# The final RMSNorm of a two-group decoder step: from feature columns to token rows

## The chip, the cores and the metric

One core of one Trainium2 chip. The metric is the device time of one execution of the whole program in microseconds (us); the median of several executions counts. Engines are named as in the profile: PE (TensorE), DVE (VectorE), ACT (ScalarE), POOL (GpSimd), SP (SyncE, which only issues DMAs here).

## What is computed

One step of a decoder layer for two groups that share the weights: a prompt of 512 tokens and 8 sample sequences with one new token each, so T = 520 tokens, model width 1024. The layer has three mixers (sparse attention, a short convolution, a linear recurrence), an output projection and a SwiGLU feed-forward of width 2816. At its very end stands the part that the change touches:

```python
xp = xp + _swiglu(_rmsnorm(xp, norm2_g[l]), w_ffn_in[l], w_ffn_out[l])
...
y_prompt = _rmsnorm(xp, final_g)     # x * rsqrt(mean(x*x, -1) + eps) * final_g, for each token
y_sample = _rmsnorm(xs, final_g)
```

All outputs are float32. Each dense product is made of three products of rounded halves (high x high, high x low, low x high), so every k step of every weight tile issues six matmuls.

## The kernel before, in words

The residual stream lives in SBUF with the features on the partitions: `xT` is [128, 8 feature tiles, 520 tokens]. Weights come in chunks of 256 output columns. For each chunk SP issues two DMAs into one of two raw buffers (`load`), ACT copies it rounded (`hi`, line 821), POOL subtracts the rounded copy (`split`, line 729), and PE multiplies (`dense`, its matmuls at line 1770). In `dense` a chunk has two output tiles, m = 0 and 1, and for each the k steps of 128 input features follow one another; a hook `between(m, k)` can put other PE work behind a k step. In an earlier stage this hook already carries turns of the same kind: `kv_turn`, lines 2037 and 2038, four 128x128 transposes and one of 8 rows between k steps.

The last stage of weights is the output product of the feed-forward, chunks `C_FO` = 70 to `C_END` = 82. An output pair is 12 chunks in two rounds of a PE loop (`pe.Fori(0, 2)`), each with j = 0 to 5: j = 0 to 2 sum over the 22 feature tiles of the hidden layer (8, 8 and 6 k steps) into the PSUM tiles D[0] and D[1], j = 3 to 5 the same for two more output tiles into the four banks of E. DVE adds each finished tile to the residual (`xT`, line 1749, semaphore `x_last`), ACT squares it (line 828) and DVE adds the square to `rstd`, which here serves as the sum of squares (line 1134).

The final norm follows the last tile, each step waiting for the one before:

- PE multiplies the sum of squares with a matrix of 1/1024 (`norm_sums(2)`), which leaves the mean of every token on all 128 partitions.
- ACT takes the square root of 128x520 (line 834), DVE the reciprocal (line 1118).
- DVE scales the eight tiles with the column of `final_g` and the token row (line 1123) into `yT`.
- PE turns `yT` by 128 tokens at a time into D[0] and D[1], then the 8 sample tokens into E (lines 2239 and 2243); ACT and DVE copy half of each turned block to `y_tok[q]` (lines 1096, 1757, 1760).
- SP stores 128 tokens with a DMA as soon as both halves are there, and the sample rows last (line 467, 2.13 MB in five DMAs).

`yT` lies in SBUF where the hidden layer's activations are still read until the last matmul.

Of the kernel before, what the change touches and what calls it, by code (L numbers as in the profile page):

```python
# [44 lines left out]
FT = D_FF // P  # L45
# [15 lines left out]
C_Q, C_KV, C_GM0, C_NSA, C_WO, C_FI, C_FO, C_END = 26, 30, 36, 40, 44, 48, 70, 82  # L61
# [17 lines left out]
def build(nc, x_prompt, x_sample, cache_kv, cache_win, state_sconv, state_lru_conv, state_lru_h, page_table,  # L79
# [4 lines left out]
    with ExitStack() as ctx:  # L84
        def sem(name):
            return ctx.enter_context(nc.semaphore(name))
# [23 lines left out]
        xT = sb("xT", [P, KT, T])  # L110
# [13 lines left out]
        g_cols = sb("g_cols", [P, 3, KT])  # L124
# [155 lines left out]
        y_tok = [over(f"y_tok{q}", [P, D_MODEL]) for q in range(QT)]  # L280
        ys_tok = over("ys_tok", [NS, D_MODEL])
        yT = over("yT", [P, KT, T])

        D = [ctx.enter_context(nc.psum_tensor(f"D{m}", [P, 2, 512], F32)) for m in range(2)]
        E = ctx.enter_context(nc.psum_tensor("E", [P, 4, 512], F32))
# [6 lines left out]
        off_blk = smalls[:, 5, 0:NS * NBLK_S]  # L292
        o_all = tmp[:, 0, 0:KVC].rearrange("p (g d) -> p g d", g=N_KV)
        o_own = tmp[:, 1, 0:2 * DH]

        x_landed = [sem(f"x_landed{q}") for q in range(QT)]
# [40 lines left out]
        v_hi = sem("v_hi")  # L338
        v_lo = sem("v_lo")
        neg_la = sem("neg_la")  # L340
        la_exp = sem("la_exp")
        mult_sq = sem("mult_sq")
        mult_ready = sem("mult_ready")
        y_sq = sem("y_sq")
        gelu_arg = sem("gelu_arg")
        gelu_tanh = sem("gelu_tanh")
# [84 lines left out]
        x_last = sem("x_last")  # L431
        y_ready = sem("y_ready")
        y_turned = sem("y_turned")
        y_evac_a = sem("y_evac_a")
        y_evac_v = sem("y_evac_v")

        block = ctx.enter_context(nc.Block())

# [24 lines left out]
        def _(sp):  # L463
            outs = [0]

            def out(dst, src):
                sp.dma_start(dst, src).then_inc(out_written, 16)
                outs[0] += 16
# [171 lines left out]
            with sp.Fori(0, 2) as i:  # L640
                for j in range(6):
                    k0, nk = ((0, KT), (KT, KT), (2 * KT, FT - 2 * KT))[j % 3]
                    load(C_FO + 6 * i + j, j % 2, wk[:, k0:k0 + nk, bass.ds(i * 2 * CW + (j // 3) * CW, CW)], nk)
            for q in range(QT):
                sp.wait_ge(y_evac_a, q + 1)
                sp.wait_ge(y_evac_v, q + 1)
                out(y_prompt[0, q * P:(q + 1) * P, :], y_tok[q][:, :])
            sp.wait_ge(y_evac_v, QT + 2)
            out(y_sample[:, 0, :], ys_tok[:, :])
            sp.wait_ge(out_written, outs[0])  # L650
            sp.wait_ge(rows_moved, 3 * 16)

# [142 lines left out]
        def pair(ap):  # L796

            return ap.rearrange("p (a c) -> p a c", a=2)
# [14 lines left out]
        def _(act):  # L813
# [16 lines left out]
            def norm(k):  # L830

                act.wait_ge(sq_summed, k)
                sums = D[0][:, :, 0:HALF] if k == 2 else E[:, 0:2, 0:HALF]
                nc.scalar.activation(pair(tmp[:, 0, :]), sums, ACT.Sqrt, bias=eps_col[:, 0:1])\
                    .then_inc(rms_done, 1)
            act.dma_start(xs_in[:, :], x_sample[:, 0, :]).then_inc(xs_landed, 16)
            for n, g in enumerate((norm1_g[0], norm2_g[0], final_g)):
# [48 lines left out]
                if ft % 2 == 1:  # L886
                    hi(4, ft // 2)
            act.wait_ge(neg_la, WT)
            nc.scalar.activation(la[:, :, :], t0[:, :, :], ACT.Exp, scale=-1.0).then_inc(la_exp, 1)
            nc.scalar.activation(lm[:, :, :], t0[:, :, :], ACT.Tanh).then_inc(la_exp, 1)  # L890
            hi(5, 0)
            act.wait_ge(mult_sq, 1)
            nc.scalar.activation(lm[:, :, :], lm[:, :, :], ACT.Sqrt).then_inc(mult_ready, 1)
            hi(5, 1)
            def mix(i, c0):

# [187 lines left out]
            for c in range(C_FO, C_END):  # L1084
                if c < C_END - 2:
                    hi((c + 2) // 2, c % 2)
                if c % 3 == (C_FO + 2) % 3:
                    for m in range(2):
                        n = (c - C_FO) // 3 * 2 + m
                        act.wait_ge(x_last, 4 + n + 1)  # L1090
                        square(2, n)
            norm(2)

            for q in range(QT):
                act.wait_ge(y_turned, q + 1)
                nc.scalar.activation(y_tok[q][:, 0:512], D[q % 2][:, 0, :], ACT.Copy).then_inc(y_evac_a, 1)

        @block.vector
        def _(dve):  # L1100
# [7 lines left out]
            def settle():  # L1108
                dve.wait_ge(vec_step, steps[0])
# [6 lines left out]
            def norm(k):  # L1116
                dve.wait_ge(rms_done, k)
                step(nc.vector.reciprocal(rstd[:, :], tmp[:, 0, :]))
                settle()
                if k < 2:  # L1120
                    return
                for ft in range(KT):
                    nc.vector.scalar_tensor_tensor(yT[:, ft, :], xT[:, ft, :], g_cols[:, k, ft:ft + 1],  # L1123
                                                   rstd[:, :], ALU.mult, ALU.mult).then_inc(y_ready, 1)

            def clear_squares():
                step(nc.vector.memset(rstd[:, :], 0.0))

            def add_square(k, ft, parity):

                n = KT * (k - 1) + ft
                dve.wait_ge(sq_done, n + 1)
                dve.wait_ge(sq_added, n)
                nc.vector.tensor_tensor(rstd[:, :], rstd[:, :], tmp[:, parity, :], ALU.add).then_inc(sq_added, 1)
# [159 lines left out]
            dve.wait_ge(la_exp, 2)  # L1294
            step(nc.vector.tensor_tensor(t0[:, :, :], la[:, :, :], la[:, :, :], ALU.mult))
            settle()

# [5 lines left out]
            dve.wait_ge(mult_ready, 1)  # L1303
            step(nc.vector.memset(lm[:, :, 0:1], 1.0))
            step(nc.vector.memset(la[:, :, 0:1], 0.0))
            settle()
# [434 lines left out]
                gated(i, 1)  # L1741

            clear_squares()
            settle()
            for n in range(KT):
# [12 lines left out]
            dve.wait_ge(y_turned, QT + 1)  # L1758
            for k in range(2):
                nc.vector.tensor_copy(ys_tok[:, k * 512:(k + 1) * 512], E[0:NS, k, :]).then_inc(y_evac_v, 1)  # L1760

        @block.tensor
        def _(pe):
            mm, turn = nc.tensor.matmul, nc.tensor.transpose

            def product(out2, lhsT, rhs, first, last):

                for a in range(2):
                    ins = mm(out2[:, a, 0:HALF], lhsT, rhs[:, a * HALF:(a + 1) * HALF], start=first, stop=last)  # L1770
                return ins
# [40 lines left out]
            def norm_sums(k):  # L1812

                pe.wait_ge(sq_added, KT * k)
                product(D[0] if k == 2 else E[:, 0:2, :], ones[:, :], rstd[:, :], True, True).then_inc(sq_summed, 1)

            for m in range(2):
# [398 lines left out]
                    dense(2 * i + b, b, KT, xgH, xgL)  # L2217
            for m in range(2):
                pe.wait_ge(tile_free[m], 1 + C_FO)
            with pe.Fori(0, 2) as i:  # L2220
                for j in range(6):
                    if j < 3:
                        pe.wait_ge(act_lo, 2 + min((j + 1) * KT, FT))
                    if j % 3 == 0:
                        pe.wait_ge(x_last, 4 * i + 2 + 2 * (j // 3))
                    outs = [D[0], D[1]] if j < 3 else [E[:, 0:2, :], E[:, 2:4, :]]
                    nk = KT if j % 3 < 2 else FT - 2 * KT
                    part = min(j % 3, 1)
                    dense(6 * i + C_FO + j, j % 2, nk, actH[part], actL[part], x0=(j % 3 - part) * KT, outs=outs,
                          first=(j % 3 == 0), last=(j % 3 == 2))  # L2230
            norm_sums(2)
            for q in range(QT):
                if q >= 2:
                    pe.wait_ge(y_evac_a, q - 1)
                    pe.wait_ge(y_evac_v, q - 1)
                for ft in range(KT):
                    if q == 0:
                        pe.wait_ge(y_ready, ft + 1)
                    ins = turn(D[q % 2][:, ft // 4, (ft % 4) * P:(ft % 4 + 1) * P], yT[:, ft, q * P:(q + 1) * P],
                               ident[:, :])  # L2240
                ins.then_inc(y_turned, 1)
            for ft in range(KT):
                ins = turn(E[0:NS, ft // 4, (ft % 4) * P:(ft % 4 + 1) * P], yT[:, ft, SEQ:T], ident[:, :])
            ins.then_inc(y_turned, 1)
# [27 lines left out]
```

## Time and profile before

| what | value |
|---|---|
| time, median of 3 runs | 1195.12 us (1194.12 to 1198.5) |
| time of the profiled execution | 1197.33 us |
| its span, first to last instruction | 1195.6 us |
| mean granted TensorE clock | 0.981 |
| busy: PE, DVE, ACT, POOL | 1134.1, 469.5, 372.5, 467.0 us |
| DMA moved in all | 126.28 MB, mean 106 GB/s |

### The profile page before, as it was taken

The page shows a single profiled execution, that of the slowest core. Times are in us where ns is not written, and L with a number is a line of the kernel's source. Part 1 is how long each engine was busy: PE and PEld are TensorE (multiplying, and loading weights), DVE is VectorE, ACT ScalarE, POOL GpSimd, SP SyncE. Part 2 cuts the span into 40 slices and gives each one's busy share as a digit, 9 for nine tenths or more (in the row PEclk, how much of TensorE's full clock was granted, in tenths as well). Part 3 has the DMA queues.
Part 4 walks back from the last instruction along what each step waited for, and adds up shares of the span by engine and source line. Part 5 has one row for each costly group of instructions (what it writes and reads, how often), then busy time and mean ns, then how long its engine had stood idle before and what let it go on. Part 6 is the DMA issues. An engine that isn't in the chain of part 4 may idle for free.

```text
span 1195.6 us, 20737 instructions
## 1 busy us (share of the span) xinstructions
PE 1134.1 (95%) x8502; PEld 1043.1 (87%) x8502; DVE 469.5 (39%) x618; ACT 372.5 (31%) x497; POOL 467.0 (39%) x265
## 2 busy tenths in 40 slices
PE   5899989999999999899899889999999999999995
PEld 5899989999999988765454579999999999999994
DVE  5586583123421230557662624352332233200115
ACT  5113433322211225255545313342322222212211
POOL 5333455555443423215511133444434344344440
PEclk9899999999999999999999989999999999999997
DMA  5532117324622223442116573223232322222201
GB/s 172 167 104 73 53 53 227 104 75 123 195 74 83 90 75 113 160 134 52 33 42 221 162 264 106 84 94 101 76 105 71 104 95 80 96 71 98 97 26 72
DMA packets 109362, 126.28 MB, mean 106 GB/s; under 512 B 10670, under 2 KB 102982, under 8 KB 107775
## 3 DMA queue, kind: packets, MB, share of 16 engines
q1 hardware_dynamic: 105784, 120.19, 32.2%
q10 hardware_dynamic: 3527, 5.39, 1.4%
q8 instruction: 35, 0.57, 0.2%
q14 instruction: 16, 0.13, 0.0%
HBM read 111.38 MB, written 16.17 MB: 107 GB/s over the span
## 4 chain that ended last, share of the span: by engine, by line
PE 75%; issue 13%; POOL 5%; DVE 3%; DMA 2%; ACT 1%; SPq 0%; ACTq 0%; POOLq 0%; DVEq 0%
PE D L1770 55%; PE E L1770 6%; PE D L2021 5%; POOL w_lo L729 4%; PE D L2006 1%; PE D L2007 1%; DMA w_raw<-in_w_in 1%; DVE nmax L1484 1%; PE E L1987 1%; PE E L2077 1%; PE E L1956 1%; DMA slot<-in_cache_win 1%; PE E L1982 0%; PE E L2037 0%; DVE yT L1123 0%
## 5 line engine op out<-in xcount | busy, mean ns | idle before, releaser
L729 POOL TENSOR_TENSOR w_lo<-w_raw,w_hi 128x1024 fp32r<-128x1024 f32 x164 | 402.0, 2473 | 565.4 <-ACT w_hi L821 544.5
L821 ACT ACTIVATE w_hi<-w_raw 128x1024 fp32r<-128x1024 f32 x164 | 164.1, 1049 | 300.1 <-PE D L1770 243.6
L1770 PE MATMUL D<-hH,w_hi 128*128 128x260 f32 x1152 | 239.9, 290 | 7.6 <-POOL w_lo L729 5.5
L1770 PE MATMUL D<-hH,w_lo 128*128 128x260 f32 x1152 | 233.5, 285 | 0.0
L1770 PE MATMUL D<-hL,w_hi 128*128 128x260 f32 x1152 | 233.5, 285 | 0.0
L1770 PEld LDWEIGHTS D<-hH,w_hi 128*128 128x128 f32 x1152 | 179.9, 191 | 12.5 <-POOL w_lo L729 5.7
L1770 PEld LDWEIGHTS D<-hL,w_hi 128*128 128x128 f32 x1152 | 179.4, 190 | 0.0
L1770 PEld LDWEIGHTS D<-hH,w_lo 128*128 128x128 f32 x1152 | 179.3, 190 | 0.0
L1770 PE MATMUL D<-onH,w_lo 128*128 128x260 f32 x816 | 164.5, 283 | 0.0
L1770 PE MATMUL D<-onH,w_hi 128*128 128x260 f32 x816 | 164.3, 282 | 0.0
L1770 PE MATMUL D<-onL,w_hi 128*128 128x260 f32 x816 | 164.2, 283 | 0.0
L1770 PEld LDWEIGHTS D<-onH,w_hi 128*128 128x128 f32 x816 | 125.9, 188 | 0.1
L1770 PEld LDWEIGHTS D<-onH,w_lo 128*128 128x128 f32 x816 | 125.8, 188 | 0.0
L1770 PEld LDWEIGHTS D<-onL,w_hi 128*128 128x128 f32 x816 | 125.4, 188 | 0.0
L2021 PE MATMUL D<-pT,vst 128*128 128x512 f32 x160 | 83.3, 605 | 2.3 <-ACT obuf L1016 2.3
L1007 ACT ACTIVATE pT<-D 128x512 f32<-128x512 f32 x80 | 47.4, 596 | 65.9 <-PE D L2007 65.8
L2006 PE MATMUL D<-qst,k 128*128 128x512 f32 x80 | 60.6, 757 | 5.4 <-issue 3.4
L779 POOL TENSOR_SCALAR_AFFINE_SELECT pT<-pT 128x512 f32<-128x512 f32 x32 | 23.6, 736 | 105.8 <-ACT pT L1007 105.8
L1484 DVE TENSOR_REDUCE nmax<-E 128x2 f32<-128x256 f32 (+3 forms) x64 | 51.1, 822 | 20.9 <-PE E L1983 13.6
L1729 DVE TENSOR_TENSOR tmp<-D,th 128x520 f32<-128x520 f32 x22 | 15.4, 699 | 88.3 <-PE D L1770 88.3
L1075 ACT ACTIVATE actH<-tmp 128x520 f32 x22 | 14.1, 640 | 93.3 <-DVE tmp L1729 93.3
L1719 DVE TENSOR_TENSOR D<-D,rstd 128x520 f32<-128x520 f32 x22 | 15.6, 707 | 64.4 <-PE D L1770 64.2
(357 smaller groups left out, 1490.8 us busy)
## 6 DMA issues: line engine op xcount, KB each, us to landing
w_raw<-in_w_in SPq DMA_DIRECT2D x64, 512.0 KB, 5.0
w_raw<-in_w_ffn_in SPq DMA_DIRECT2D x44, 512.0 KB, 4.1
slot<-in_cache_kv SPq DMA_DIRECT2D x64, 128.0 KB, 2.6
w_raw<-in_w_ffn_out SPq DMA_DIRECT2D x16, 512.0 KB, 4.0
rows_b<-rnorm_d SPq DMA_DIRECT2D x8, 512.0 KB, 4.7
w_raw<-in_w_nsa_out SPq DMA_DIRECT2D x8, 512.0 KB, 9.0
slot<-in_cache_win SPq DMA_DIRECT2D x16, 256.0 KB, 4.6
w_raw<-in_w_o SPq DMA_DIRECT2D x8, 512.0 KB, 4.2
```

What stands on the lines that cost most here:

```text
L729: nc.gpsimd.tensor_tensor(wl[b][:, x], raw[b][:, x], wh[b][:, x].bitcast(F32), ALU.subtract)\
L779: nc.gpsimd.affine_select(out=p, in_=p, compare_op=ALU.is_ge, fill=0.0, base=0, pattern=[[0, R], [1, P]], channel_multiplier=-1).then_inc( ...
L821: nc.scalar.activation(wh[b][:, x], raw[b][:, x], ACT.Copy).then_inc(hi_done, 1)
L1007: nc.scalar.activation(pT[t % 4][:, :, :].rearrange("p r x -> p (r x)"), D[0][:, t % 2, :], ACT.Exp)\
L1075: nc.scalar.activation(actH[part][:, bass.ds(2 * i - part * KT + m, 1), :].squeeze(1), tmp[:, m, :], ACT.Copy).then_inc(act_hi, 1)
L1484: nc.vector.reduce_max(nmax[:, g % 2, a, :, qi % 2, h], src, AX.X, negate=True).then_inc(nmax_done, 1)
L1719: nc.vector.tensor_tensor(o, o, pair(rstd[:, :]), ALU.mult).then_inc(ffn_gate, 1)
L1729: nc.vector.tensor_tensor(pair(tmp[:, m, :]), D[m][:, :, 0:HALF], pair(th[:, m, :]), ALU.mult)\
L1770: ins = mm(out2[:, a, 0:HALF], lhsT, rhs[:, a * HALF:(a + 1) * HALF], start=first, stop=last)
L1956: mm(E[:, ft % 4, :], vbig[:, ft * P:(ft + 1) * P], pcT[:, :, :].rearrange("p q x -> p (q x)"), start=True, stop=True).then_inc(cmp_out, 1)
L2006: mm(out, k1[b][:, br, ks], qst[b][:, qi, :, :].rearrange("p r x -> p (r x)"), start=True, stop=False)
L2021: mm(D[1][:, i % 2, :], vst[g % 2][:, br, kt, :], pT[t % 4][:, :, :].rearrange("p r x -> p (r x)"), start=(kt == 0), stop=(kt == qi)).then ...
```

## The change

The final norm is taken token by token, with tokens on the partitions. The unscaled residual tiles are turned while the last output products still run: a turn of tile n writes the four blocks of 128 tokens into one bank of D[0] and the 8 sample tokens into a bank of D[1], alternating two banks. DVE multiplies the turned tile with `g_row`, `final_g` spread over all partitions by a DMA from SP, into `y_tok` and `ys_tok` (`weigh`). Turns 0 to 3 stand behind k = 0, 2, 4, 6 of the second tile of chunk j=3 of the second round, turns 4 and 5 in the first tile of j=4, turn 6 behind k=3 of the second tile of j=5, and turn 7 follows the last matmul. The PE loop is written out for this. The sums of squares come as one column for each block of 128 tokens (`token_sums`, one matmul per block with the squares as weights and one column of 1/1024), first for the sum of tiles 0 to 6, then added for tile 7 from its own square. Square root and reciprocal are then of 128x5. Whole rows are scaled last, in place: DVE takes blocks 0 and 2 and the sample rows, SP stores them; ACT takes blocks 1 and 3 and stores them from its own queue. A dummy square root behind ACT's first weight copies of this stage loads the activation table. `y_tok`, `ys_tok` and `g_row` lie where the input of the feed-forward was, free by then. Two pairs of semaphores are merged into one each, as is said in the diff.

```diff
+        y_tok = over("y_tok", [P, QT, D_MODEL])
         ys_tok = over("ys_tok", [NS, D_MODEL])
-        yT = over("yT", [P, KT, T])
+        g_row = over("g_row", [P, D_MODEL])
...
+        rms_y, rstd_y = smalls[:, 1, 0:QT + 1], smalls[:, 2, 0:QT + 1]
...
-        la_exp = sem("la_exp")
+        la_act = sem("la_act")
-        mult_ready = sem("mult_ready")
...
# SP
-            for q in range(QT):
-                sp.wait_ge(y_evac_a, q + 1)
-                sp.wait_ge(y_evac_v, q + 1)
-                out(y_prompt[0, q * P:(q + 1) * P, :], y_tok[q][:, :])
-            sp.wait_ge(y_evac_v, QT + 2)
+            sp.wait_ge(pe_done, 2 * C_FO)
+            sp.dma_start(g_row[:, :], final_g.unsqueeze(0).to_broadcast([P, D_MODEL])).then_inc(g_landed, 16)
+            for n, q in enumerate((0, 2)):
+                sp.wait_ge(y_scaled_v, n + 1)
+                out(y_prompt[0, q * P:(q + 1) * P, :], y_tok[:, q, :])
+            sp.wait_ge(y_scaled_v, 3)
             out(y_sample[:, 0, :], ys_tok[:, :])
-            sp.wait_ge(out_written, outs[0])
+            sp.wait_ge(out_written, outs[0] + 2 * 16)
...
# ACT
+                if c == C_FO:
+                    nc.scalar.activation(smalls[:, 3, 0:1], eps_col[:, :], ACT.Sqrt)
-            norm(2)
-
-            for q in range(QT):
-                act.wait_ge(y_turned, q + 1)
-                nc.scalar.activation(y_tok[q][:, 0:512], D[q % 2][:, 0, :], ACT.Copy).then_inc(y_evac_a, 1)
+            act.wait_ge(sq_summed, 2)
+            nc.scalar.activation(rms_y[:, 0:QT], E[:, :, 0:1].squeeze(2), ACT.Sqrt, bias=eps_col[:, 0:1]).then_inc(rms_done, 1)
+            nc.scalar.activation(rms_y[0:NS, QT:QT + 1], D[0][0:NS, 0, 0:1], ACT.Sqrt, bias=eps_col[0:NS, 0:1])\
+                .then_inc(rms_done, 1)
+            act.wait_ge(y_ready, 1)
+            act.wait_ge(y_weighed, KT)
+            for n, q in enumerate((1, 3)):
+                nc.scalar.activation(y_tok[:, q, :], y_tok[:, q, :], ACT.Copy, scale=rstd_y[:, q:q + 1])\
+                    .then_inc(y_scaled_a, 1)
+                act.wait_ge(y_scaled_a, n + 1)
+                act.dma_start(y_prompt[0, q * P:(q + 1) * P, :], y_tok[:, q, :]).then_inc(out_written, 16)
...
# DVE
-                for ft in range(KT):
-                    nc.vector.scalar_tensor_tensor(yT[:, ft, :], xT[:, ft, :], g_cols[:, k, ft:ft + 1],
-                                                   rstd[:, :], ALU.mult, ALU.mult).then_inc(y_ready, 1)
...
+            step(nc.vector.memset(rms_y, 1.0))
...
+            def weigh(n):
+                dve.wait_ge(y_turned, n + 1)
+                x = slice(n * P, (n + 1) * P)
+                nc.vector.tensor_tensor(y_tok[:, :, x], D[0][:, n % 2, :].rearrange("p (q x) -> p q x", q=QT),
+                                        g_row[:, x].unsqueeze(1).to_broadcast([P, QT, P]), ALU.mult)
+                nc.vector.tensor_tensor(ys_tok[:, x], D[1][0:NS, n % 2, 0:P], g_row[0:NS, x], ALU.mult)\
+                    .then_inc(y_weighed, 1)
+
+            for n in range(6):
+                last_tile(n)
                 if n > 0:
                     add_square(2, n - 1, (n - 1) % 2)
-            add_square(2, KT - 1, 1)
-            norm(2)
-            for q in range(QT):
-                dve.wait_ge(y_turned, q + 1)
-                nc.vector.tensor_copy(y_tok[q][:, 512:1024], D[q % 2][:, 1, :]).then_inc(y_evac_v, 1)
-            dve.wait_ge(y_turned, QT + 1)
-            for k in range(2):
-                nc.vector.tensor_copy(ys_tok[:, k * 512:(k + 1) * 512], E[0:NS, k, :]).then_inc(y_evac_v, 1)
+            add_square(2, 5, 1)
+            dve.wait_ge(g_landed, 64)
+            for n in range(6):
+                weigh(n)
+            last_tile(6)
+            add_square(2, 6, 0)
+            weigh(6)
+            last_tile(7)
+            weigh(7)
+            dve.wait_ge(rms_done, 3)
+            nc.vector.reciprocal(rstd_y, rms_y).then_inc(y_ready, 1)
+            dve.wait_ge(y_ready, 1)
+            dve.wait_ge(y_weighed, KT)
+            for q in (0, 2):
+                nc.vector.tensor_scalar(y_tok[:, q, :], y_tok[:, q, :], rstd_y[:, q:q + 1], None, ALU.mult)\
+                    .then_inc(y_scaled_v, 1)
+            nc.vector.tensor_scalar(ys_tok[:, :], ys_tok[:, :], rstd_y[0:NS, QT:QT + 1], None, ALU.mult)\
+                .then_inc(y_scaled_v, 1)
...
# PE
-            with pe.Fori(0, 2) as i:
-                for j in range(6):
...
-            norm_sums(2)
...
+            def turn_y(n):
+                pe.wait_ge(x_last, 4 + max(n + 1, 6))
+                if n >= 2:
+                    pe.wait_ge(y_weighed, n - 1)
+                for q in range(QT):
+                    turn(D[0][:, n % 2, q * P:(q + 1) * P], xT[:, n, q * P:(q + 1) * P], ident[:, :])
+                turn(D[1][0:NS, n % 2, 0:P], xT[:, n, SEQ:T], ident[:, :]).then_inc(y_turned, 1)
+
+            def turns_within(j):
+                def between(m, k):
+                    if (j, m) == (3, 1) and k % 2 == 0:
+                        turn_y(k // 2)
+                    if (j, m) == (4, 0) and k % 4 == 0:
+                        turn_y(4 + k // 4)
+                    if (j, m, k) == (5, 1, 3):
+                        turn_y(6)
+                return between
+
+            for j in range(6):
+                output_chunk(0, j)
+            for j in range(6):
+                output_chunk(1, j, turns_within(j))
+
+            def token_sums(sq, qs, first):
+                for q in qs:
+                    out, w = (E[:, q, 0:1], slice(q * P, (q + 1) * P)) if q < QT else (D[0][0:NS, 0, 0:1], slice(SEQ, T))
+                    ins = mm(out, sq[:, w], ones[:, 0:1], start=first, stop=not first)
+                return ins
+
+            pe.wait_ge(sq_added, 2 * KT - 1)
+            token_sums(rstd, (0, 1), True)
+            turn_y(7)
+            pe.wait_ge(y_weighed, KT - 1)
+            token_sums(rstd, (2, 3, 4), True)
+            pe.wait_ge(sq_done, 2 * KT)
+            token_sums(tmp[:, 1, :], range(QT + 1), False).then_inc(sq_summed, 1)
```

`output_chunk` is the body of the former loop, with `between` handed to `dense`; `last_tile` is the former first half of DVE's loop (line 1749). `ident` is the identity, `ones` a matrix of 1/1024.

## Rows read from the trace of the kernel before

**Rows 1.** The page: busy time of the engines, and ACT's group of weight copies.
```profile
PE 1134.1 (95%) x8502; PEld 1043.1 (87%) x8502; DVE 469.5 (39%) x618; ACT 372.5 (31%) x497; POOL 467.0 (39%) x265
...
L821 ACT ACTIVATE w_hi<-w_raw 128x1024 fp32r<-128x1024 f32 x164 | 164.1, 1049 | 300.1 <-PE D L1770 243.6
```

**Rows 2.** The chain in order of time, 1100 to 1197: start, length, what.
```profile
1141.29 31.74 PE E L1770 x264
...
1173.05 0.71 DVE xT L1749
...
1175.22 1.16 PE D L1770 x4
...
1176.40 0.70 ACT tmp L834
...
1177.12 3.41 DVE rstd L1118
...
1180.56 5.47 DVE yT L1123 x8
...
1186.08 5.12 PE D L2239 x25
```

**Rows 3.** Stretches of the end: length, busy PE, PEld, DVE, ACT, POOL, PEclk, DMA share, GB/s.
```profile
1188.20:1189.50 1.30, 1.30 (x8) 1.30 (x7) 0.69 (x1) 0.60 (x1) 0.00 (x0) 0.50 0.99 400
1191.50:1194.30 2.80, 0.57 (x6) 0.24 (x3) 1.71 (x3) 0.33 (x1) 0.00 (x0) 1.00 0.99 382
1194.30:1195.60 1.30, 0.00 (x0) 0.00 (x0) 0.00 (x0) 0.00 (x0) 0.00 (x0) 1.00 0.08 16
```

**Rows 4.** Timeline of PE in the stage with turns between k steps: start, length, instructions.
```profile
432.25 0.41 PE L1770 MATMUL D<-hH,w_hi 128*128 128x260 f32 x2
...
432.98 0.40 PE L1770 MATMUL D<-hH,w_hi 128*128 128x260 f32 x2
...
438.03 0.60 PE L2037 MATMUL E<-ident,vT 128*128 128x128 f32 x4
...
439.30 0.60 PE L2037 MATMUL E<-ident,vT 128*128 128x128 f32 x4
...
443.42 0.63 PE L2037 MATMUL E<-ident,kT 128*128 128x128 f32 x4
```

**Rows 5.** Three lines of DVE: times of one in ns (min/median/max), first and last start.
```profile
L1719 DVE TENSOR_TENSOR D<-D,rstd x22: 707/707/708, 799.3 to 1033.1; 128x520 f32<-128x520 f32 x22
...
L1134 DVE TENSOR_TENSOR rstd<-rstd,tmp x16: 690/1118/1951, 755.8 to 1174.5; 128x520 f32<-128x520 f32 x16
...
L1291 DVE TENSOR_SCALAR t<-t,spl x4: 480/1552/2661, 134.9 to 140.4; 128x520 f32<-128x520 f32 x4
```

**Rows 6.** Timeline of SP's queue: the last loads of weights and the first stores, merged.
```profile
1116.17 23.54 SPq L476 DMA_DIRECT2D w_raw<-in_w_ffn_out  x6
1187.38 4.95 SPq L467 DMA_DIRECT2D out_y_prompt<-y_tok  x4
```

**Rows 7.** The page's DMA issues: count, KB each, median us to landing.
```profile
w_raw<-in_w_nsa_out SPq DMA_DIRECT2D x8, 512.0 KB, 9.0
```

**Rows 8.** Timeline of the kernel's first 12 us, ACT and DVE.
```profile
2.47 1.28 ACT L840 ACT_TABLE_LOAD   x1 [2.47 <-issue]
...
11.22 0.30 ACT L849 ACTIVATE rs<-ssq,eps_col 128x5 f32<-128x5 f32 x1
...
11.55 0.19 DVE L1152 RECIPROCAL rs<-rs 128x5 f32<-128x5 f32 x1 [1.32 <-ACT rs L849]
```

**Rows 9.** Timeline of PE: float32 products with 8 columns, 128x128 weights.
```profile
668.31 0.61 PE L2150 MATMUL E<-k_new,q_all 128*128 128x8 f32 x4
668.78 0.37 PE L2152 MATMUL E<-offseq,ident 128*128 128x8 f32 x2
```

**Rows 10.** Stretches with the granted clock (the column behind POOL's).
```profile
431.00:458.00 27.00, 26.72 (x222) 25.69 (x221) 9.04 (x16) 11.06 (x18) 5.24 (x3) 1.00 0.19 46
...
1177.00:1178.00 1.00, 0.00 (x0) 0.00 (x0) 0.88 (x1) 0.09 (x1) 0.00 (x0) 0.50 0.00 0
```

More of the change, by code:

```diff
@@ L279, in build @@
         over = Region(rest, end)
-        y_tok = [over(f"y_tok{q}", [P, D_MODEL]) for q in range(QT)]
+        y_tok = over("y_tok", [P, QT, D_MODEL])
         ys_tok = over("ys_tok", [NS, D_MODEL])
-        yT = over("yT", [P, KT, T])
+        g_row = over("g_row", [P, D_MODEL])
         D = [ctx.enter_context(nc.psum_tensor(f"D{m}", [P, 2, 512], F32)) for m in range(2)]
@@ L433, in build @@
         y_turned = sem("y_turned")
-        y_evac_a = sem("y_evac_a")
-        y_evac_v = sem("y_evac_v")
+        y_weighed = sem("y_weighed")
+        y_scaled_a = sem("y_scaled_a")
+        y_scaled_v = sem("y_scaled_v")
         block = ctx.enter_context(nc.Block())
@@ L832, in norm @@
                 act.wait_ge(sq_summed, k)
-                sums = D[0][:, :, 0:HALF] if k == 2 else E[:, 0:2, 0:HALF]
-                nc.scalar.activation(pair(tmp[:, 0, :]), sums, ACT.Sqrt, bias=eps_col[:, 0:1])\
+                nc.scalar.activation(pair(tmp[:, 0, :]), E[:, 0:2, 0:HALF], ACT.Sqrt, bias=eps_col[:, 0:1])\
                     .then_inc(rms_done, 1)
@@ L888, in _ @@
             act.wait_ge(neg_la, WT)
-            nc.scalar.activation(la[:, :, :], t0[:, :, :], ACT.Exp, scale=-1.0).then_inc(la_exp, 1)
-            nc.scalar.activation(lm[:, :, :], t0[:, :, :], ACT.Tanh).then_inc(la_exp, 1)
+            nc.scalar.activation(la[:, :, :], t0[:, :, :], ACT.Exp, scale=-1.0).then_inc(la_act, 1)
+            nc.scalar.activation(lm[:, :, :], t0[:, :, :], ACT.Tanh).then_inc(la_act, 1)
             hi(5, 0)
             act.wait_ge(mult_sq, 1)
-            nc.scalar.activation(lm[:, :, :], lm[:, :, :], ACT.Sqrt).then_inc(mult_ready, 1)
+            nc.scalar.activation(lm[:, :, :], lm[:, :, :], ACT.Sqrt).then_inc(la_act, 1)
             hi(5, 1)
@@ L1119, in norm @@
                 settle()
-                if k < 2:
-                    return
-                for ft in range(KT):
-                    nc.vector.scalar_tensor_tensor(yT[:, ft, :], xT[:, ft, :], g_cols[:, k, ft:ft + 1],
-                                                   rstd[:, :], ALU.mult, ALU.mult).then_inc(y_ready, 1)
             def clear_squares():
@@ L1293, in _ @@
             y_tile(0)
-            dve.wait_ge(la_exp, 2)
+            dve.wait_ge(la_act, 2)
             step(nc.vector.tensor_tensor(t0[:, :, :], la[:, :, :], la[:, :, :], ALU.mult))
@@ L1302, in _ @@
             step(nc.vector.scalar_tensor_tensor(t1[:, :, :], t1[:, :, :], 1.0, xc[:, :, :], ALU.add, ALU.mult))
-            dve.wait_ge(mult_ready, 1)
+            dve.wait_ge(la_act, 3)
             step(nc.vector.memset(lm[:, :, 0:1], 1.0))
@@ L1743, in _, with last_tile @@
             clear_squares()
+            step(nc.vector.memset(rms_y, 1.0))
             settle()
-            for n in range(KT):
+            def last_tile(n):
                 pairs, m = n // 2, n % 2
@@ L1814, in norm_sums @@
                 pe.wait_ge(sq_added, KT * k)
-                product(D[0] if k == 2 else E[:, 0:2, :], ones[:, :], rstd[:, :], True, True).then_inc(sq_summed, 1)
+                product(E[:, 0:2, :], ones[:, :], rstd[:, :], True, True).then_inc(sq_summed, 1)
             for m in range(2):
@@ L2219, in _ @@
                 pe.wait_ge(tile_free[m], 1 + C_FO)
-            with pe.Fori(0, 2) as i:
-                for j in range(6):
[L2222 to L2230, printed above, removed]
@@ L2231, in _ @@
-            norm_sums(2)
[L2232 to L2241, printed above, removed]
@@ L2242, in _, with output_chunk @@
-            for ft in range(KT):
-                ins = turn(E[0:NS, ft // 4, (ft % 4) * P:(ft % 4 + 1) * P], yT[:, ft, SEQ:T], ident[:, :])
-            ins.then_inc(y_turned, 1)
+            def output_chunk(i, j, between=None):
+                if j < 3:
+                    pe.wait_ge(act_lo, 2 + min((j + 1) * KT, FT))
+                if j % 3 == 0:
+                    pe.wait_ge(x_last, 4 * i + 2 + 2 * (j // 3))
+                outs = [D[0], D[1]] if j < 3 else [E[:, 0:2, :], E[:, 2:4, :]]
+                nk = KT if j % 3 < 2 else FT - 2 * KT
+                part = min(j % 3, 1)
+                dense(6 * i + C_FO + j, j % 2, nk, actH[part], actL[part], x0=(j % 3 - part) * KT, outs=outs,
+                      first=(j % 3 == 0), last=(j % 3 == 2), between=between)
```

## The prediction

> **What bounds the kernel now.** I read the page first: TensorE is busy for 95% of the span [rows 1]. So the place to look is the end, where it has no matmuls of weights left. The chain in order of time [rows 2] shows it: the last dense matmul ends at 1173.03, and 22.6 us follow in which each engine waits for the one before it: residual tile, square, sum of squares, `ones` product, square root, reciprocal 3.4 us, scaling 5.5 us, turns 5.1 us and those of the sample rows, their copies. The DMA view of the same stretch [rows 3] shows the stores of y: 2.13 MB in all, the first flowing at 1188.2, 0.8 us after its issue at 1187.4 [rows 6], and 1.3 us from the last bytes to the end of the span. While bytes flow, the DMA engines are 99% busy, at 382 to 400 GB/s. The stores lie half under the turns.
>
> The sum is made against the profiled execution: span 1195.6 us, time 1197.33 us. The median of the runs is 1195.12 us; I take the difference in span over to it.
>
> **Part 1, turns inside the last output pair (added before the last matmul).** Turns 0 to 3 come in chunk j=3, 4 and 5 in j=4, 6 in j=5: seven before the last dense matmul. Each is four 128x128 transposes and one of 8 rows. The same thing stands in the trace in lines 2037 and 2038, straight-line code between k steps of `dense` [rows 4]: a k step without a turn takes 0.73 us (432.25 to 432.98), with one 1.27 (438.03 to 439.30). So one turn costs 0.54 us and seven cost 3.8 us, all on the path: the last dense matmul ends at 1176.85. Bounds: nothing below 0.54 is seen; above, 0.84, the step in which PE also waited 0.3 us for an evacuation (443.42), which is 5.9 us in all. I take 0.54, as our turns are two k steps apart or more.
>
> That evacuation, `weigh`, is hidden by this: a turn plus two k steps is 2.0 us, and DVE needs about 0.71 for a product that reads 128x520 from PSUM [rows 5], and for the small one of 8 rows less than that again, 1.4 at most. Sums of squares, with all operands in SBUF, took from 0.69 to 1.95, longest beside POOL's subtractions, but the products from PSUM 707 to 708 ns in all 22, and `weigh` reads PSUM. With two buffers in D, PE waits only if `weigh` is a further 2 us late. Behind `weigh` on DVE stand tiles 6 and 7. `weigh(6)` starts after the turn at k=3 of the last pass, with two k steps (1.45 us) left, so even at 1.4 us it ends as tile 7 comes due; if that cover is gone, the overrun is added.
>
> **Part 2, the load of g_row.** SP issues it behind the last weight load, at 1139.7 [rows 6]; SP has nothing else queued until the stores. The slowest kind of load of the same 512 KB landed after 9.0 us [rows 7], so by 1149. `weigh(0)` could start at 1148.1, and PE needs it only at turn 2, near 1151.6. Cost nothing, and at the high bound still nothing. It delays no weights that are due: the last chunk's load was issued just before it, and PE first has the whole chunk j=4 to work through.
>
> **Part 3, the sqrt table.** The load (1.28 us) moves to a dummy behind ACT's first weight copies of the output stage, where ACT waits for PE's next chunk anyway; before, it lay under the sum of squares. At the kernel's start one load was followed by Sqrt, Square and Copy with no second [rows 8], so it stays loaded. Cost nothing, gain nothing. Unrolling the PE loop: the first half ran straight through for its first time without a gap, and so did the code of rows 4; nothing. The renamed semaphores, one memset: nothing.
>
> **Part 4, the new tail, from 1176.85.** The residual tile 7 takes 0.75 with its hand-overs [rows 2], to 1177.6. Two sums over tokens run on PE meanwhile. Then PE has one turn (0.54) and eight sums with one column. A float32 product is recorded as two passes: four passes with 8 columns took 0.47 us from start to start [rows 9], so 0.12 a pass; 16 passes make 1.9, and 0.15 for the end of the last: 1180.2. Bounds for a pass: nothing (-1.9 us), as one column is less than eight, and 0.29, a pass of 260 columns, four in 1.16 [rows 2] (+2.7 us). ACT's square of tile 7, 520 columns like the root's 0.70 [rows 2], is done by then. Two square roots: 0.30 for one with 128x5 [rows 8], 0.2 more for the second, which overlaps: 1180.7. Bounds 0.3 and, at 0.7 each (128x520, rows 2), 1.4. The reciprocal of 128x5 is 0.19 [rows 8]: 1180.95. This replaces the reciprocal of 3.4.
>
> Scaling of rows: DVE with a pointer and all in SBUF took 0.48 us at best for 520 columns [rows 5], 1.5 and more beside POOL, which is idle by now; less the 0.19 that even five columns take, this is 0.56 ns a column, so 0.76 for 1024: 1181.7. Bounds 0.48 and 1.36 (twice a sum of squares' 0.69 at best, less what is fixed). ACT takes about 1.05 for 1024 columns [rows 1], then issues its store: 1182.2. Even if DVE were at its bound, ACT's store would start the flow 0.4 us later.
>
> SP issues the store of rows 0 at 1181.8; bytes flow from 1182.6. Rows 1, 2 and 3 follow by 1182.3, 1182.6 and 1183.8, faster than the engines drain 0.52 MB (1.3 us each). So 2.13 MB at 390 GB/s, between the 382 and 400 of rows 3, take 5.4 us: 1188.0, and with 1.3 us of end, **1189.3**. This is the new bound: DMA, no engine. Before, 22.6 us followed the last matmul; now 3.8 + 12.4 = 16.2. **The span is 6.3 us shorter**: 1190.9 against 1197.33, on the median 1188.8.
>
> The stores come from two queues, and here a rule speaks. The rows show the DMA engines 99% busy under a single queue's stores [rows 3], so I give no gain in rate. The Trainium skill, page "DMA: Bandwidth & Descriptors", section "Issuing engines are not separate DMA queues", says the same thing against the change's last point: DMAs of several issuers run on the same 16 engines and interleave, and only issue time is saved. By that rule the trace agrees, and the sum stays 1188.8; without it the flow could halve.
>
> **Rivals.**
> The half clock: the granted clock fell from 1.00 to 0.50 by 1177, when TensorE had been idle for 2.2 us after 1173.03 and then worked 1.1 [rows 2, 10]; turns then took 0.205 us each (25 in 5.12 [rows 2]) where rows 4 show 0.11. Now only 0.3 us of idle lie before turn 7. If the clock falls at the last matmul all the same, the turn and 16 passes take about 2.3 us more: 1191.1. One-column passes (+2.7), square roots (+0.9) or row scaling (+0.6, capped at +0.4 by ACT's store) at their high bounds give +0.4 to +2.7, and I put them in one case. For: the tail has seven hand-overs that no row shows in this form. Against: each was 0.02 to 0.05 us in rows 2. A sentence beside it: the Trainium skill, "TensorE: Matmul & The Clock Gate", section "Part 1: The HAM clock gate", says that recent activity holds the clock up, and the trace agrees: it fell by 1177, in the first pause of this stage.
> Two queues do add: flow in 2.7 us, 1186.1. Against: 99% busy.
> Slower: PE stalls in the last pair, at turn 2, because `weigh` is late, and the clock falls there. The 21 us of matmuls from 1151.6 on then run at half speed: 1188.8 + 21 = 1210. It decides from 12.3 us at half clock (6.3 to lose, 6.0 to be 0.5% slower). Against: the stretch of rows 4, with the same turns and two stalls of 0.3 us, ran at clock 1.00 [rows 10].
> The change does nothing like it says: if the stores already set the end, only the gap would go. Rows 6 deny it: SP issues no store before 1187.4, and the chain [rows 2] runs through the compute until then.
>
> **How the numbers follow.** About 0.5% (6.0 us) is what a measurement of this kernel can tell from no change, and the forecast gain of 6.3 is hardly over it. Chances: forecast, within 1 us, 0.60; the case of clock and hand-overs 0.31; two queues add 0.05; PE stalls 0.04, of which 0.02 slower. Of the forecast 0.5 lie on the faster side and 0.1 below the bound; with the 0.05, faster 0.55; same 0.42; slower 0.03. Low end 1186.4, near the faster flow and one-column passes at their low bound (1186.9), high end 1192.2: the high bounds of passes and clock, and run-to-run difference of about 0.7.
>
> **What would show it.** The last matmul of E near 1176.8, at clock 1.00, and no idle of PE before turns 1 to 6. Square roots near 1180.2, ACT and DVE scaling from 1181. DMA flowing without a gap from 1182.6 to 1188, at 385 to 400 GB/s. Wrong if: a turn costs over 0.6 us; PEclk is 0.5 between 1177 and 1180; the flow has gaps or another rate; g_row lands after 1150.

## The result and the profile after

The changed kernel takes 1190.02 us in the median of 6 runs (1185.96 to 1190.82), the kernel before 1195.19 us beside it (1194.03 to 1198.5). The ratio is 0.9942 with a 95% interval of 0.9923 to 0.9961, that is 6.9 us less, with an interval of 4.7 to 9.2; by the medians it is 5.2 us less. The forecast was 1188.8 us, 6.3 us less. The profiled execution took 1189.87 us, with a span of 1188.1 us.

The chain of work in order of time, from the last output pair on (start, length, what; PE's line of `dense` is now 1797), stands against [rows 2]:

```profile
1139.93 6.25 PE E L1797 x52
1146.18 0.44 PE D L2263 x4
1146.61 0.11 PE D L2264
1146.72 1.46 PE E L1797 x12
...
1173.80 1.45 PE E L1797 x12
1175.25 0.02 issue
1175.28 0.71 DVE xT L1755
1175.99 0.04 issue
1176.03 0.66 PE D L2263 x4
1176.69 0.11 PE D L2264
1176.80 0.34 PE E L2284 x4
1177.14 0.12 PE D L2284 x2
1177.26 0.98 PE E L2284 x8
1178.25 0.14 PE D L2284 x2
...
1178.57 0.24 ACT smalls L1097
...
1178.84 0.20 DVE smalls L1780
...
1179.07 1.16 ACT y_tok L1102
1180.22 0.02 issue
1180.25 0.37 ACTq L1105
```

A turn stands in the chain with 0.44 + 0.11 us between the matmuls of E, and nothing waits around it. Behind the last matmul, the 3.4 us of a reciprocal and 5.5 us of scaling are gone; a turn of 0.77 us, sums of 1.6 us, two roots, 0.20 us of reciprocal and the scaling of whole rows stand there instead.

The whole comparison can be put into three numbers, read in DVE's timeline from the residual tiles (line 1749 before, 1755 after). Tile 5 frees D, tile 7 is the last; "tail" is from the start of tile 7 to the end of the span. The spans are given to a tenth of a microsecond, so a tail is good to about 0.05 us. The two rows of after:

```profile
1139.72 0.70 DVE L1755 SCALAR_TENSOR_TENSOR xT<-D,xT 128x520 f32<-128x520 f32 x1 [2.15 <-PE D L1797]
...
1175.28 0.70 DVE L1755 SCALAR_TENSOR_TENSOR xT<-E,xT 128x520 f32<-128x520 f32 x1 [0.56 <-PE E L1797]
```

| | start of tile 5 | tiles 5 to 7 | tail |
|---|---|---|---|
| before | 1141.32 | 31.73 | 22.55 |
| after | 1139.72 | 35.56 | 12.82 |

The seven turns cost 3.83 us, the tail is 9.73 us shorter: 5.9 us less where the change is. The other 1.6 us of the spans' 7.5 lie before tile 5.

The end, in stretches (columns as in [rows 3]):

```profile
1178.00:1179.00 1.00, 0.37 (x5) 0.26 (x4) 0.16 (x1) 0.40 (x2) 0.00 (x0) 1.00 0.00 0
1179.00:1180.00 1.00, 0.00 (x0) 0.00 (x0) 0.96 (x3) 0.93 (x1) 0.00 (x0) 0.67 0.00 0
1180.00:1181.00 1.00, 0.00 (x0) 0.00 (x0) 1.00 (x2) 0.55 (x2) 0.00 (x0) 0.50 0.32 127
1181.00:1182.00 1.00, 0.00 (x0) 0.00 (x0) 0.13 (x1) 0.81 (x1) 0.00 (x0) 0.50 0.99 393
1182.00:1183.00 1.00, 0.00 (x0) 0.00 (x0) 0.00 (x0) 0.00 (x0) 0.00 (x0) 0.50 1.06 414
1183.00:1184.00 1.00, 0.00 (x0) 0.00 (x0) 0.00 (x0) 0.00 (x0) 0.00 (x0) 0.50 1.03 401
1184.00:1185.00 1.00, 0.00 (x0) 0.00 (x0) 0.00 (x0) 0.00 (x0) 0.00 (x0) 0.50 1.10 340
1185.00:1186.00 1.00, 0.00 (x0) 0.00 (x0) 0.00 (x0) 0.00 (x0) 0.00 (x0) 0.50 0.87 348
1186.00:1187.00 1.00, 0.00 (x0) 0.00 (x0) 0.00 (x0) 0.00 (x0) 0.00 (x0) 0.50 0.28 111
```

The clock is 1.00 until PE has nothing left to do, and falls when it no longer matters. From 1182 on no engine works but the DMA engines: the stores are the bound, in one piece, where [rows 3] had them half under the turns.

### The profile page after: what moved, and what is told of

Same layout as the page of the kernel before. It is cut to its first block, busy times and chain, and to the rows that moved or that the text cites. A ratio compares the mean times of both kernels' runs of the same rounds, so it can differ in the third digit from the quotient of the medians.

```text
span 1188.1 us, 20750 instructions
## 1 busy us (share of the span) xinstructions
PE 1130.3 (95%) x8518; PEld 1042.0 (88%) x8518; DVE 467.5 (39%) x623; ACT 372.3 (31%) x497; POOL 467.1 (39%) x265
## 4 chain that ended last, share of the span: by engine, by line
PE 75%; issue 13%; POOL 5%; DVE 2%; DMA 2%; ACT 1%; SPq 0%; ACTq 0%; POOLq 0%; DVEq 0%
PE D L1797 55%; PE E L1797 6%; PE D L2048 5%; POOL w_lo L731 4%; PE D L2033 1%; PE D L2034 1%; DMA w_raw<-in_w_in 1%; DVE nmax L1488 1%; PE E L2014 1%; PE E L2104 1%; PE E L1983 1%; PE E L2009 0%; DMA slot<-in_cache_win 0%; PE E L2064 0%; DVE obuf L1512 0%
```

## The experiments

All start from the changed kernel, except three that start from the kernel before. The three numbers of each profile, in one table; each row is one execution:

| run | tile 5 | tiles 5 to 7 | tail | what differs |
|---|---|---|---|---|
| e1_one_queue | 1135.82 | 35.54 | 12.34 | SP issues all stores |
| e2_turns_twice | 1138.46 | 39.40 | 12.84 | turns 0 to 6 twice |
| e3_turns_after | 1136.63 | 31.73 | 19.54 | all turns after the last matmul |
| e4_half_stored | 1135.79 | 35.54 | 9.67 | blocks 2 and 3 not stored |
| e6_after_again | 1137.66 | 35.54 | 12.90 | the changed kernel |
| e7_no_dummy | 1137.89 | 35.54 | 12.87 | no dummy square root |
| v2_one_queue | 1138.73 | 35.54 | 11.13 | three edits on the tail |
| e5_before_again | 1142.29 | 31.73 | 23.78 | the kernel before |
| e8_loop_unrolled | 1137.66 | 31.73 | 22.51 | before, PE's loop written out |
| e9_before_warm | 1140.48 | 31.73 | 21.89 | before, PE kept busy |

### What a turn costs inside the output products, and what the place is worth

```diff
-                for q in range(QT):
-                    turn(D[0][:, n % 2, ...], xT[:, n, ...], ident[:, :])
-                turn(D[1][0:NS, n % 2, 0:P], xT[:, n, SEQ:T], ident[:, :]).then_inc(y_turned, 1)
+                for again in range(2 if n < 7 else 1):
+                    ...
+                ins.then_inc(y_turned, 1)
```

> Each of the turns 0 to 6 is issued twice, with the same result. Theory (a turn costs PE 0.54 us and nothing hides it; weigh stays hidden): the stretch from residual tile 5 to residual tile 7 grows from 35.56 us to 39.4, the tail behind it is unchanged at 12.8. Rival (a part of the 3.83 us is the waits around the turns or the changes between the two kinds of matmul): it grows by less than 3, to under 38.6.

It grew by 3.84 us, to 39.40, and the tail stayed. So the price is the five transposes themselves, 0.55 us a turn, not waits around them or the change from one kind of matmul to the other.

```diff
-                output_chunk(1, j, turns_within(j))
+                output_chunk(1, j)
-            turn_y(7)
+            for n in range(KT):
+                pe.wait_ge(x_last, 4 + KT)
+                turn_y(n)
# DVE: last_tile(6), add_square(2, 6, 0), last_tile(7), then weigh(0) to weigh(7)
```

> No turn inside the output products; turns 0 to 7 and their products with g_row follow the last matmul. Theory (inside, DVE's 0.96 us per tile are hidden and PE's 0.54 are paid; outside, DVE's 0.96 set the pace): residual tile 5 to tile 7 is back at 31.73 us; the tail grows from 12.8 to about 19.3 (turn 7 ends some 6.5 us later), in sum 2.7 us more than the change. Rival (turns are as dear inside as out, 0.54 each, so the place is indifferent): the tail grows by only 3.8 us, the sum is the same.

The stretch is back at 31.73 us and the tail is 19.54, 6.7 us more than with the turns inside: in sum 2.9 us more than the change, against 2.7 expected. So of the 5.9 us, 3.0 come from the new form of the norm (the kernel before has 31.73 + 22.55 us, this run 31.73 + 19.54) and 2.9 from the place of the turns. In DVE's timeline the products with `g_row` now follow one another closely (first the big one from PSUM, then that of the 8 rows):

```profile
1169.92 0.69 DVE L1761 TENSOR_TENSOR y_tok<-D,g_row 128x512 f32<-128x512 f32 x1 [0.86 <-PE D L2262]
1170.53 0.27 DVE L1763 TENSOR_TENSOR ys_tok<-D,g_row 8x128 f32<-8x128 f32 x1
1170.73 0.67 DVE L1761 TENSOR_TENSOR y_tok<-D,g_row 128x512 f32<-128x512 f32 x1
...
1176.12 0.68 DVE L1761 TENSOR_TENSOR y_tok<-D,g_row 128x512 f32<-128x512 f32 x1
1176.72 0.27 DVE L1763 TENSOR_TENSOR ys_tok<-D,g_row 8x128 f32<-8x128 f32 x1
```

Eight take 7.1 us, 0.88 each, where the theory had 0.96: the small product overlaps the end of the big one, and two tiles whose turns are both ready start 0.81 us apart. Nor is it DVE alone that sets the pace. With two buffers, every second turn waits until a product has freed its buffer, as the chain shows:

```profile
1170.95 0.63 PE D L2261 x4
...
1171.72 0.69 DVE y_tok L1761
1172.41 0.20 DVE ys_tok L1763
...
1172.74 0.63 PE D L2261 x4
```

That is 1.8 us for two tiles. Seven products more behind the last matmul are 6.2 of the 6.7 us (the last one starts 7.76 us into the tail, against 1.56); the rest is that the sums, which wait for the product of tile 6, end later behind it. Inside the output products this runs under PE's matmuls, and only PE's 0.55 us per tile is paid. This is what putting the turns there wins.

### The stores

```diff
-            for n, q in enumerate((0, 2)):
-                sp.wait_ge(y_scaled_v, n + 1)
-                out(y_prompt[0, q * P:(q + 1) * P, :], y_tok[:, q, :])
+            sp.wait_ge(y_scaled_v, 1)
+            out(y_prompt[0, 0:P, :], y_tok[:, 0, :])
...
-                act.dma_start(y_prompt[0, q * P:(q + 1) * P, :], y_tok[:, q, :]).then_inc(out_written, 16)
+                if q == 1:
+                    act.dma_start(y_prompt[0, q * P:(q + 1) * P, :], y_tok[:, q, :]).then_inc(out_written, 16)
```

The output leaves out blocks 2 and 3 of y_prompt.

> Rows of blocks 2 and 3 (1.05 MB) are scaled but not stored, so half of y_prompt is left out. Theory (from the first store on, the end is set by bytes at 390 to 400 GB/s): the tail falls by 2.6 to 2.8 us, from 12.8 to about 10.1. Rival (the end is set by the latency of a store and the scaling before it): it falls by less than 1 us.

The tail fell by 3.15 us, to 9.67: the stores' bytes set the end. It is more than the 2.6 to 2.8 us expected, which took the full rate for the whole flow; 1.05 MB in 3.15 us are 333 GB/s. The rate of the changed kernel's flow falls off in its last 2 us (the stretches of the end above), and its end is looked at next.

```diff
+            for q, scaled, n in ((0, y_scaled_v, 1), (1, y_scaled_a, 1), (2, y_scaled_v, 2)):
+                sp.wait_ge(scaled, n)
+                out(y_prompt[0, q * P:(q + 1) * P, :], y_tok[:, q, :])
+            ...
-                act.dma_start(y_prompt[0, q * P:(q + 1) * P, :], y_tok[:, q, :]).then_inc(out_written, 16)
```

> Only the issuing queue differs: ACT still scales rows 1 and 3, but SP issues all five stores. Theory (the 16 DMA engines are the bound, one queue fills them): from the residual tile 7 to the end of the span 12.8 us as with two queues, within 0.5, bytes flowing at 385 to 400 GB/s. Rival (two queues add rate, one alone is slower): the flow of 2.13 MB takes clearly longer than 5.6 us, the tail 13.8 us or more. Second rival (the two queues end unevenly, since with them the rate fell to about 200 GB/s in the last microsecond): with one queue the rate holds to the last bytes and the tail is 0.3 to 0.6 us shorter, 12.3.

The tail is 12.34 us, 0.5 less than with two queues, as the second rival had it (the theory's "within 0.5" just allows for it too). From the issue of the first store to the end of the span it is 7.8 us here (1175.93 to 1183.7) and 8.3 with two queues (1179.85 to 1188.1), again 8.3 in e2_turns_twice (1182.43 to 1190.7), in e3_turns_after (1179.56 to 1187.9) and in the other two profiles with two queues; v2_one_queue below has 7.8 again. Over most of the flow the rates are the same.

```profile
1176.70:1180.10 3.40, 0.00 (x0) 0.00 (x0) 0.52 (x1) 0.64 (x1) 0.00 (x0) 0.50 1.00 394
1180.10:1181.10 1.00, 0.00 (x0) 0.00 (x0) 0.00 (x0) 0.00 (x0) 0.00 (x0) 0.50 1.08 344
1181.10:1182.10 1.00, 0.00 (x0) 0.00 (x0) 0.00 (x0) 0.00 (x0) 0.00 (x0) 0.50 0.89 356
1182.10:1183.10 1.00, 0.00 (x0) 0.00 (x0) 0.00 (x0) 0.00 (x0) 0.00 (x0) 0.50 0.25 98
```

That is one queue; two had 393 in 3.4 us, then 340, 348 and 111 (above). The difference is in the very end, and there the rival's reason is borne out. These are the stretches from 6.75 us after the first store's issue on, first with two queues, then with one:

```profile
1186.60:1187.20 0.60, 0.00 (x0) 0.00 (x0) 0.00 (x0) 0.00 (x0) 0.00 (x0) 0.50 0.07 27
1187.20:1188.10 0.90, 0.00 (x0) 0.00 (x0) 0.00 (x0) 0.00 (x0) 0.00 (x0) 0.50 0.00 0
```

```profile
1182.68:1183.28 0.60, 0.00 (x0) 0.00 (x0) 0.00 (x0) 0.00 (x0) 0.00 (x0) 0.50 0.02 7
1182.83:1183.69 0.86, 0.00 (x0) 0.00 (x0) 0.00 (x0) 0.00 (x0) 0.00 (x0) 0.50 0.00 0
```

With two queues a DMA share of 0.07, which is one of the 16 engines, goes on for 0.6 us at 27 GB/s when the others are done; with one queue nothing flows after 1182.83. This uneven end is about 0.4 of the 0.5 us. Why one engine lags with two queues stays open. The Trainium skill, page "DMA: Bandwidth & Descriptors", section "Issuing engines are not separate DMA queues", has it that several issuers save only issue time. In rate the runs agree; there was little issue time to save here, as the DMA share was 1.00 for the first 3.4 us of the flow with one queue too.

### The table load and the unrolled loop

```diff
-                if c == C_FO:
-                    nc.scalar.activation(smalls[:, 3, 0:1], eps_col[:, :], ACT.Sqrt)
```

> Without the dummy square root, so that the activation table is loaded at the first real one. Theory (the load of 1.28 us starts when ACT has squared tile 7 and is over before PE's sums, 1.7 us later): tail 12.8, no change. Rival (the load stands in the tail): the tail grows by 1.3, or by what the sums do not cover.

The tail is 12.87 us. ACT's timeline shows the load between the square of tile 7 and the first root, 0.46 us before it is needed:

```profile
1174.16 0.64 ACT L830 ACTIVATE tmp<-xT 128x520 f32<-128x520 f32 x1 [4.23 <-DVE xT L1753]
1174.82 1.28 ACT L1094 ACT_TABLE_LOAD   x1
1176.56 0.26 ACT L1094 ACTIVATE smalls<-E,eps_col 128x4 f32<-128x4 f32 x1 [0.46 <-PE D L2282]
```

So the dummy wins nothing here, as expected before the run.

```diff
 # the kernel before
-            with pe.Fori(0, 2) as i:
+            for i in range(2):
                 for j in range(6):
```

> The kernel before with PE's loop over the two halves of the output stage written out, nothing else. Theory (the step into the loop costs PE 0.44 us, 1.28 idle before its first matmul where the changed kernel has 0.84): from the reciprocal of the second norm to the first residual tile 277.5 us, where the two traces of the kernel before have 277.9 and the changed ones 277.46 to 277.48; the tail stays 22.5 to 23.8. Rival (that difference comes from ACT's or DVE's side of the change): 277.9.

From the reciprocal at 792.48 to the first residual tile at 1069.94 it is 277.46 us, and e9_before_warm, which has the loop, is back at 277.94 (794.83 to 1072.77): the 0.44 us are the loop's. PE's first matmul of the stage in PE's timeline, first of the kernel before, then with the loop written out (in brackets the idle time before it):

```profile
1045.85 0.50 PE L1770 MATMUL D<-actH,w_hi 128*128 128x260 f32 x2 [1.28 <-DVE tmp L1729]
```

```profile
1042.20 0.48 PE L1770 MATMUL D<-actH,w_hi 128*128 128x260 f32 x2 [0.84 <-issue]
```

### The clock in the old tail, and what lies before tile 5

> The kernel before once more. Theory (the place at which the last output pair starts differs between executions by weights' and rows' transfers long before it, not by the change): its tail is 22.55 us again within 0.1 and the stretch of tiles 5 to 7 31.73, but tile 5 comes anywhere between 1136 and 1142, as it did in the five traces of the changed kernels (1135.8 to 1139.7) and this one's first (1141.3). Rival (the change also makes the part before earlier): tile 5 is at 1141 or later again.

The tail was 23.78 us, not 22.55 within 0.1: a miss, and a telling one. The same product of the sum of squares took 1.16 us in the first profile [rows 2] and 2.11 in this one. The first profile's clock around the product, then this one's chain and clock:

```profile
1175.00:1176.00 1.00, 0.78 (x4) 0.68 (x4) 0.16 (x1) 0.72 (x1) 0.00 (x0) 1.00 0.00 0
1176.00:1177.00 1.00, 0.36 (x2) 0.00 (x0) 0.00 (x0) 0.60 (x1) 0.00 (x0) 0.96 0.00 0
```

```profile
1176.18 2.11 PE D L1770 x4
...
1188.00 5.37 PE D L2239 x25
```

```profile
1175.00:1176.00 1.00, 0.00 (x0) 0.00 (x0) 0.90 (x2) 0.98 (x2) 0.00 (x0) 0.97 0.00 0
1176.00:1177.00 1.00, 0.82 (x2) 0.72 (x3) 0.13 (x1) 0.69 (x1) 0.00 (x0) 0.50 0.00 0
```

Here the granted clock fell just before the product, in PE's pause of 2.1 us behind the last matmul; in the first profile it fell just after it. In both the turns then ran at half clock, so the old tail had the half-clock case in it; what differs between executions is whether the product is caught too. Tile 5 came at 1142.29, as the rival said. In the next two runs, e8_loop_unrolled and e9_before_warm, which differ from the kernel before only behind 1040 us, it came at 1137.66 and 1140.48, so "at 1141 or later" does not hold. But it is not shown that the change leaves the part before alone. The reciprocal of the second norm, which lies before everything that was moved, comes at 792.5 to 796.7 us in the four profiles with the old code in front of it (mean 794.9) and at 790.6 to 794.5 in the eight with the new (mean 792.4): 2.5 us apart in the mean, with ranges that overlap. In what the engines do and wait for there, the code differs only by a merged pair of semaphores (`la_act`), and no run takes that back. One place where the executions differ is the stretch from 690 to 704 us, where PE waits for cached rows: its granted clock was 0.68 and 0.59 in the two profiles of the kernel before, 0.93 in e8_loop_unrolled, 0.81 in e9_before_warm, and between 0.71 and 0.99 in those of the changed kernels.

```diff
 # the kernel before
+            def filler(n):
+                for _ in range(n):
+                    mm(D[1][:, 0, 0:HALF], wh[0][:, 0:P], actH[0][:, 0, 0:HALF], start=True, stop=True)
+            filler(14)
             norm_sums(2)
+            filler(36)
...
+                        filler(3 if ft else 0)       # before each turn of block 0 but the first
```

> The kernel before with matmuls that nobody reads in PE's pauses of the final norm (14 before the sum product, 36 behind it, 3 between the first turns), so that the granted clock stays at 1.00. Theory (the low clock is a small part of the old tail, since behind faster turns the stores become the bound: the first is issued 14.3 us into the tail as before, 0.8 + 5.5 + 1.3 follow): the tail is 21.8 to 22.0, 0.6 to 0.8 us less than the shorter of the two seen; the turns take 0.11 us each. Rival (the clock is most of what the change wins): the tail falls by more than 2 us, to 20.5 or less.

The tail was 21.89 us, with the clock at 1.00 until PE was done and the last 25 turns in 3.1 us in place of 5.1. The stores then followed one another and became the bound, with a DMA share of 1.02 at 402 GB/s from 1187.6 to 1192. So the clock was worth 0.7 us of the old tail against the first profile and 1.9 against the second, and little of what the change wins.

### Three more edits on the tail

```diff
# sums over tokens: rounded operands (sumR, sq7R), one pass
-  out E[:, q, 0:1] ...  mm(out, sq[:, w], ones[:, 0:1], ...)
+  out E[:, q, 0:2] ...  mm(out, sq[:, w], ones_r[:, 0:2], ...)        # squares are taken with scale 1/32
# DVE scales and SP stores block 0 in two halves; SP issues all stores
+            for q, x in ((0, slice(0, 512)), (0, slice(512, 1024)), (2, slice(0, 1024))):
```

> Three edits on the changed kernel: the sums over tokens use rounded operands, one pass in place of two; the first block is scaled and stored in two halves of 512 columns; SP issues all stores. Theory (each takes its part of the tail: eight passes of 0.1 us, 0.27 us of the first scaling, 0.48 us as the one queue showed): tail 12.8 - 0.8 - 0.3 - 0.5 = 11.3 us. Rival (one of them only moves the wait, to the product of tile 7 with g_row or to the rate of the stores): tail 12.0 or more.

The tail is 11.13 us. The eight passes behind turn 7 end 1.40 us after the start of that turn (1175.02 to 1176.42), where sixteen took 2.36. So the sums give 0.96 us. The first store is issued 0.51 us after the scaling starts instead of 0.78 (1177.10 to 1177.61, against 1179.07 to 1179.85), and from there to the end it is 7.8 us instead of 8.3: the parts add up to the 1.7 us by which the tail is shorter. Timed side by side, six runs each, this version took 1186.87 us (ratio to the kernel before 0.9924, 0.9897 to 0.9951), the changed kernel 1187.8 and the kernel before 1196.48:

> The changed kernel, timed in five rounds. Theory (3.83 us more before the last matmul, 9.73 us less behind it): 5.9 us less than before, ratio 0.9951, plus what lies in the part before it, which the last rounds put at up to 1.5 us more; tail 12.8. Rival (the first rounds' 5.2 by medians or 6.9 by ratio were not drift): the ratio stays under 0.9945.

Its ratio was 0.9929 (0.9903 to 0.9954), below 0.9945 as the rival had it, though the interval reaches above that. The 1.7 us between the two versions in the tail are plain in the profiles, but their intervals overlap widely: no timing here tells them apart. Nor do they tell the 5.9 us of the theory, or 6.3 with the loop, from the 8.5 that this ratio gives, since the interval reaches from 5.5 to 11.6 us.

## Why the prediction was right

The mechanism held part by part. That the whole came out so near is partly luck, as two terms missed by 0.4 us in opposite directions: the tail (part 4) and the loop (part 3).

**Part 1, the turns.** Forecast 3.8 us by rows 4, measured 3.83, and 3.84 again when doubled. No stall at any turn: DVE had the product of turn 0 done at 1147.7, turn 1 began at 1148.0 in the other bank and turn 2, which needs this one, at 1150.0.

**Part 2, g_row.** Issued by SP at 1138.33 in the profile of after, and the first `weigh` ran at 1146.83, right behind its turn at 1146.01: it waited for nothing. The cover held.

**Part 3.** The table load was worth nothing either way (e7). The unrolling was costed at nothing by the rows inside the loop; the step into it was not looked at, and it wins 0.44 us (e8). That is the one term of the sum that was missed, though the trace had a row with PE's 1.28 us of idle. The merged semaphores were put at nothing too, and no run tests that.

**Part 4, the tail.** Forecast 12.4 us, measured 12.82. The turn and the sums behind tile 7 took 2.36 us (forecast 2.6): the turn 0.77, not 0.54, behind a pause of 0.46, and the sums 1.59, not 2.05, as a pass with one column takes 0.10 us, not 0.12. The roots took 0.43 (0.5), the reciprocal 0.2, the first scaling on DVE 0.7 (0.76). The first store was issued 4.6 us into the tail (forecast 5.0). From that issue to the end it was 8.25 us where 7.5 were forecast: about 0.5 of it is what the second queue costs (e1), the rest that the rate sank to 340 to 350 GB/s and below before the end. The prediction had named another rate than 385 to 400 GB/s as a sign of being wrong, and for the last 2 us it was one. So the tail is made of an error of 0.4 us one way and one of 0.75 us the other.

**The rivals.** The half clock did not come in the new tail, whose pause before turn 7 is only 0.5 us long; it was in the old one instead (e5, e9), which makes the change's gain larger in some executions, not smaller. Two queues do not add: they cost 0.5 us. PE did not stall, and the clock was 1.00 in the whole last pair with its turns. Small slips in the working change nothing: 31 k steps of 0.73 us, the matmuls behind turn 2, are 22.6 us and not 21, so the stall case would have been near 1211; and 6.3 us off 1197.33 is 1191.0.

So the change is faster by 5.9 us in the tail and the turns and 0.44 us at the loop, 6.3 us in all, and by up to 1.2 us more where the old product of the sum of squares ran at half clock. The measured 4.7 to 9.2 us of the first timing contain that, and the 5.5 to 11.6 of the second. The forecast case was "within 1 us" of 1188.8: the median, 1190.02, is 1.2 us off, and the gain by ratio, 6.9 us, is 0.6 off. Whether the gain is over the 0.5% that the prediction took as its line is not told by the first timing, whose interval is 0.39 to 0.77%. Whether anything more is won before tile 5 is not settled: the profiles scatter there by 6.5 us (1135.8 to 1142.3).

## What to carry to other kernels

Work that must follow the last product is worth moving under the products even at full price on the busiest engine, if it takes another engine's slower share with it: 0.55 us of PE per tile under the products stood in for 0.88 us per tile behind them, and the place of the turns was worth 2.9 us in all (e3). Shrink what a whole chain waits for to the size of its information: one mean per token is 128x5, not 128x520, and the reciprocal falls from 3.4 to 0.2 us. Then look at bytes: once 2.1 MB of stores stand alone at the end, what is left to win is to start them sooner and to end them evenly. Three edits did so for 1.7 us (v2_one_queue). Storing a part of the rows under the products, for example by finishing the last pair by halves of the tokens, was not tried.

## What the runs showed that was not expected

- The same kernel's tail was 22.55 and 23.78 us in two executions, by when the clock fell around PE's pause of 2.1 us: before or after a product that takes 1.16 us at full clock and took 2.11 at half.
- Two issuing queues for four stores of 0.5 MB and a small one ended 0.5 us later than one, at the same rate over most of the flow: one DMA engine went on alone for 0.6 us.
- The step into a PE loop at the start of a stage cost 0.44 us over written-out code.
- A float32 product with one column and 128x128 weights takes two passes of 0.10 us. With rounded operands and two columns it is one pass, eight in 0.63 us.
